# Attention weights: product with a diagonal of reciprocal sums instead of a multiplication and a transpose

## The reference

```
def _attend(q, parts, sink):
    scale = q.shape[-1] ** -0.5
    logits = []
    for k_, v_, bias in parts:
        s = jnp.einsum('bkgqd,bksd->bkgqs', q, k_).astype(jnp.float32) * scale
        if bias is not None:
            s = s + bias
        logits.append(s)
    ...
    p = jax.nn.softmax(jnp.concatenate(logits, axis=-1), axis=-1)
    out, off = None, 0
    for k_, v_, _ in parts:
        n = k_.shape[2]
        o = jnp.einsum('bkgqs,bksd->bkgqd', p[..., off:off + n].astype(v_.dtype), v_)
        out = o if out is None else out + o
        off += n
    return out
```

## Time and profile before

| | us |
|---|---|
| Median of 3 runs | 1862.6 (1861.91 to 1864.54) |
| The profiled execution, its own time | 1861.61 |
| Its span, first to last instruction | 1859.8 |
| TensorE busy | 1809.1 (97%) |
| DVE busy | 1341.2 (72%) |
| ACT busy | 981.0 (53%) |
| POOL busy | 178.7 (10%) |

### The profile page before, as it was taken

How to read it: one execution, slowest core, us unless ns; L and a number is a source line. 1 busy time by engine, 2 the same in 40 slices (tenths; PEclk the granted TensorE clock), 3 DMA queues, 4 the chain that set the end, 5 groups by cost and what they waited for, 6 DMA issues and landing times.

```text
span 1859.8 us, 27382 instructions
## 1 busy us (share of the span) xinstructions
PE 1809.1 (97%) x11100; PEld 1500.4 (81%) x11100; DVE 1341.2 (72%) x1973; ACT 981.0 (53%) x1470; POOL 178.7 (10%) x154
## 2 busy tenths in 40 slices
PE   5999999999999989999999999999999999999998
PEld 2988877797888767888977778888888786878888
DVE  3865677668897566998656688966765776769984
ACT  2754445545674454776344466744644445447663
POOL 2100121001000113000011210002100210020001
PEclk8999999999999999999999999999999999999999
DMA  9565656867555767665584766556655657645542
GB/s 368 191 233 200 204 215 227 313 230 282 235 195 189 267 223 294 246 228 199 186 303 171 292 271 264 188 184 249 227 183 190 233 179 281 237 163 200 192 176 86
DMA packets 72527, 418.12 MB, mean 225 GB/s; under 512 B 12176, under 2 KB 18696, under 8 KB 24144
## 3 DMA queue, kind: packets, MB, share of 16 engines
q1 hardware_dynamic: 54288, 392.98, 56.7%
q10 hardware_dynamic: 18112, 23.38, 3.9%
HBM read 405.35 MB, written 10.95 MB: 224 GB/s over the span
## 4 chain that ended last, share of the span: by engine, by line
PE 87%; DVE 5%; issue 2%; ACT 2%; DMA 2%; POOL 2%; POOLq 0%; DVEq 0%; ACTq 0%; SPq 0%
PE ps L586 18%; PE ps L608 9%; PE ps L643 9%; PE ps L589 9%; PE ps L568 6%; PE ps L624 5%; PE ps L646 4%; PE ps L571 3%; PE ps L685 3%; PE ps L554 3%; PE ps L556 3%; PE ps L555 3%; DMA raw<-in_stream 2%; PE ps L894 1%; PE ps L655 1%
## 5 line engine op out<-in xcount | busy, mean ns | idle before, releaser
L471 DVE TENSOR_TENSOR spl_lo<-raw,spl_hi 128x1024 fp32r<-128x1024 f32 x556 | 687.2, 1260 | 185.3 <-ACT spl_hi L460 184.2
L460 ACT ACTIVATE spl_hi<-raw 128x1024 fp32r<-128x1024 f32 x556 | 573.8, 1053 | 295.9 <-PE ps L646 111.0
L586 PE MATMUL ps<-H,spl_hi 128*128 128x512 f32 x1408 | 445.1, 398 | 3.4 <-DVE H L1760 3.4
L589 PEld LDWEIGHTS ps<-H,spl_lo 128*128 128x128 f32 x1408 | 265.2, 188 | 62.7
L589 PE MATMUL ps<-H,spl_lo 128*128 128x256 f32 x1408 | 277.2, 278 | 0.0
L586 PEld LDWEIGHTS ps<-H,spl_hi 128*128 128x128 f32 x1408 | 215.0, 189 | 14.6 <-issue 14.6
L643 PE MATMUL ps<-G,spl_hi 128*128 128x512 f32 x528 | 165.8, 395 | 0.0
L568 PE MATMUL ps<-B,spl_hi 128*128 128x512 f32 x512 | 160.9, 396 | 0.0
L554 PE MATMUL ps<-H,spl_hi 128*128 128x256 f32 x512 | 148.0, 289 | 6.0 <-DVE H L1760 4.5
L555 PE MATMUL ps<-H,spl_hi 128*128 128x256 f32 x512 | 145.8, 285 | 0.0
L556 PE MATMUL ps<-H,spl_lo 128*128 128x256 f32 x512 | 145.8, 285 | 0.0
(11 more groups left out here) (248 smaller groups left out, 2893.5 us busy)
## 6 DMA issues: line engine op xcount, KB each, us to landing
raw<-in_stream SPq DMA_DIRECT2D x374, 1024.0 KB, 4.9
out_new_C<-c_stage ACTq DMA_DIRECT2D x16, 512.0 KB, 3.8
ada_b<-in_ada_b ACTq DMA_DIRECT2D x4, 768.0 KB, 9.6
E<-rows_out ACTq DMA_DIRECT2D x8, 256.0 KB, 4.3
Em<-rows_out ACTq DMA_DIRECT2D x8, 256.0 KB, 4.6
x<-in_x ACTq DMA_DIRECT2D x1, 1024.0 KB, 11.9
wide<-rows_out ACTq DMA_DIRECT2D x8, 128.0 KB, 4.7
cache<-in_na_cache ACTq DMA_DIRECT2D x1, 1024.0 KB, 8.8
```

Source lines behind the costliest of these rows:

```text
L460: act.activation(spl_hi[m % SPL][:, :], raw[r % RAW][:, h * HALF:(h + 1) * HALF], ACT.Copy).then_inc(S["hi_done"], 1)
L471: dve.tensor_tensor(spl_lo[m % SPL][:, :], raw[r % RAW][:, h * HALF:(h + 1) * HALF], spl_hi[m % SPL][:, :].bitcast(F32), ALU.subtract).the ...
L586: pe.matmul(banks[:, b * 512:(b + 1) * 512], spl_hi[m % SPL][:, c], H[:, kk * 512:(kk + 1) * 512], start=kk == 0, stop=False, skip_group_c ...
L589: mm = pe.matmul(banks[:, b * 512:b * 512 + TOK], spl_lo[m % SPL][:, c], H[:, kk * 512:kk * 512 + TOK], start=False, stop=kk == KD - 1, sk ...
```

## The change

The division by the sums no longer happens in a pass over the weights. DVE writes `diag`, four 128 x 128 diagonal matrices with `rsum` of one head each on the diagonal (the identity, broadcast over four heads, times `rsum`, broadcast over 128 columns). `weights(u)` on TensorE replaces each transpose of a block of `Ea` by the matrix product of that block, as stationary operand, with the head's diagonal as moving operand: the block transposed, its columns scaled. GpSimd's part in attention is gone, and its semaphore `pn_done` is now raised by DVE. There is one `diag`, so the reciprocal of unit u waits also for `pt_mm`, the end of unit u-1's products on TensorE. `diag` takes 2 KB that nothing else used in attention.

```diff
--- before.py
+++ after.py
@@ -353,6 +353,7 @@
     vrow = sb("vrow", NS * D, F32, rA + 16 * KB)
     rope_t = sb("rope_t", 512, F32, rA + 28 * KB)
     rope_u = sb("rope_u", 512, F32, rA + 30 * KB)
+    diag = sb("diag", 4 * T, F32, rA + 26 * KB)
     qT = sb("qT", KD * TOK, F32, rB)
     kT = sb("kT", KD * 3 * T, F32, rB + 8 * KB)
     cache = sb("cache", 2 * D, F32, rB + 20 * KB)
@@ -971,8 +972,10 @@
                         pe.wait_ge(S["pt_d"], w // 2)
                     for b in range(1 + s):
                         for p in range(4):
-                            o = (4 * b + p) * T
-                            mm = pe.transpose(ACC[2 + b][:, p * T:(p + 1) * T], Ea[s][:, o:o + T], ident)
+                            c = 4 * b + p
+                            mm = pe.matmul(ACC[2 + b][:, p * T:(p + 1) * T], Ea[s][:, c * T:(c + 1) * T],
+                                           diag[:, c // (1 + s) * T:(c // (1 + s) + 1) * T], start=p == 0, stop=p == 3,
+                                           skip_group_check=True)
                     mm.then_inc(S["pt_mm"], 1)
 
                 def values(u):
@@ -2110,7 +2113,11 @@
                         link.wait()
                     if w:
                         dve.wait_ge(S["pn_done"], w)
+                        dve.wait_ge(S["pt_mm"], w)
                     dve.reciprocal(rsum[:, :], sums[:, :]).then_inc(S["rsum_done"], 1)
+                    dve.wait_ge(S["rsum_done"], w + 1)
+                    dve.tensor_tensor(v3(diag[:, :], T), ident.unsqueeze(1).to_broadcast([P, 4, T]),
+                                      rsum[:, :].unsqueeze(2).to_broadcast([P, 4, T]), ALU.mult).then_inc(S["pn_done"], 1)
 
                 def weights(u):
                     dve.wait_ge(S["pt_mm"], 8 * a + u + 1)
@@ -2386,13 +2393,6 @@
                         chain(pool.tensor_scalar(var[:, :], v3(mv[:, :], 2)[:, :, 1], 1.0, EPS, ALU.mult, ALU.add))
                         chain.wait()
                         pool.tensor_tensor(rstd[:, :], var[:, :], half_pow[:, :], ALU.pow).then_inc(S["root_done"], 1)
-                else:
-                    for u in range(8):
-                        width = (1 + u % 2) * T
-                        pool.wait_ge(S["rsum_done"], 8 * (i - 1) + u + 1)
-                        ev = v3(Ea[u % 2][:, 0:4 * width], width)
-                        pool.tensor_tensor(ev, ev, rsum[:, :].unsqueeze(2).to_broadcast([P, 4, width]),
-                                           ALU.mult).then_inc(S["pn_done"], 1)
                 norm(2 * i + 1)
 
             norm(2 * DEPTH, shift=False)
```

## The result

| | before | after |
|---|---|---|
| Median (6 runs each, same chip) | 1862.29 (1860.7 to 1864.84) | 1868.94 (1866.47 to 1872.4) |
| Ratio | | 1.0035 [1.0024, 1.0045] |
| The profiled execution | 1861.61 | 1872.4 |

The account below looks back on a forecast made before the run. TensorE was taken to bound the kernel, with a DVE and ACT chain pacing swa from about 665 to 693 us. swa +4.6 and na -0.7 gave +3.9 on the profiled execution, median 1866.5 us; stated range 1861.5 to 1870.

Parts of the forecast that it names:

- the forecast's own range: Whole kernel: 1864.7 to 1868.3 us, from the end of na 1 us either way and the diagonal 0.1 us.
- the case in which the clock falls: Rival, chance 0.25: TensorE's clock still falls at na's end, newly in swa, or both; 1867.7 to 1869.4 us.
- The product: TensorE, both layers: each transpose made a true product costs 0.114 us more, 10.9 us in all if nothing hides it.
- The rival of the four transposes: TensorE, both layers: a true product costs four transposes, 0.436 us, adding 20.3 us, total 1882.9; chance 0.02.
- The diagonal: DVE, 16 multiplications of 0.69 us, each moving what follows by about 0.73; swa's scores of unit 6 2.3 us later.
- The rival in which DVE's own waits hide the diagonals: swa: DVE's idle between units absorbs the diagonals, swa +0.8 us, total 1862.7, no change; chance 0.15.
- GpSimd gone: Both layers: weights ready 0.3 or 1.2 us sooner after the reciprocal; DVE regains 0.54, 0.39 and 0.58 us.
- The new wait: Reciprocal waiting for the previous unit's products: costs nothing in swa, about 0.25 us at unit 6 in na.
- the prediction's own sign: The prediction is wrong if a reciprocal waits for TensorE by more than 0.3 us in several units.
- The clock in swa: Rival's part for swa: the clock newly falls behind waits of 1.6, 1.3 and 1.4 us, costing 1.7; clock rival's chance 0.25.
- The main case: The forecast itself, chance 0.48: swa +4.6 us without a clock fall, na -0.7, total 1866.5 us.
- The end of na: Unit 7's products start 0.3 us sooner; the clock stays up, worth 1.7 us, of which 1.2 remain after tiles.

Follow-up runs that it names:

- e4: From the changed kernel: GpSimd instead of DVE writes the diagonal and takes the wait for the previous unit's products; 1865.52 us against 1862.69, ratio 1.0018.
- e3: From the changed kernel: TensorE transposes again, DVE still writes the diagonal but it is unused, softmax left undivided; 1862.05 us against 1862.69, ratio 1.0000.
- e5: From the changed kernel: five unread products on TensorE in each of two idle stretches of swa; 1866.93 us against 1863.69, ratio 1.0022.
- e8: From the kernel before: GpSimd's multiplication moved to DVE in na alone, transposes kept; 1861.35 us against 1863.69, ratio 0.9986.
- e2: From the changed kernel: two diagonal buffers in turn, so a reciprocal waits for the products of two units ago; 1868.55 us against 1862.69, ratio 1.0034.
- e10: From the kernel with DVE's multiplication in na alone: wide units multiplied in two halves, TensorE starting after the first; 1861.6 us against 1862.40, ratio 0.9997.
- e1: The changed kernel run and profiled again, nothing altered; 1869.55 us against 1862.69 for the kernel before, ratio 1.0036.
- e7: From the changed kernel: modulation tiles at the end of na transfer only half their data; 1869.1 us against 1863.69, ratio 1.0032.
- e11: The kernel before with GpSimd's multiplication moved to DVE in na alone, run again on another chip; 1861.05 us against 1862.40, ratio 0.9994.
- e6: From the kernel before: transposes of the weights become true products with the identity, GpSimd still multiplies; 1871.71 us against 1863.69, ratio 1.0038.
- e9: From the changed kernel: no diagonal or product; DVE multiplies the weights in place in both layers, TensorE transposes; 1864.68 us against 1862.40, ratio 1.0014.

## Why the prediction was right, and where it was not

The forecast was 1866.5 in a range to 1870, "slower" the likeliest side; measured 1868.94. That lies above the forecast's own range (1868.3) and inside the stated one only because this was stretched over the case in which the clock falls.

**The product: right.** 0.114 us more for each was taken from L788 against L794. Sixteen records take 1.87 to 1.98 us from start to start of what follows, 0.12 a record, so a product takes about twice the transpose's 0.11 to 0.13, and 20 of them cost 2.27 us in e4. The Trainium skill (TensorE: Matmul & The Clock Gate, Terms) has transpose mode four times faster for fp32. The runs show twice, for these operands as for L788's. The rival of the four transposes is out.

**The diagonal: right.** 0.69 us, and 2.5 us of chain up to the scores of unit 6 in e3, 2.38 in e5, against 2.3. The rival in which DVE's own waits hide the diagonals is out by the same number.

**GpSimd gone: right in kind.** nm is 0.16 to 0.17 everywhere. The 0.57 that na's block at 990 was to win is the step of -0.58 there in e8 and e3. In after it is -0.45: the block starts without idle, straight behind unit 1's products and values, so they did not quite fit before it; at the next scores the shift is -0.35.

**The new wait: right in what it costs.** By the prediction's own sign it was wrong, as three reciprocals wait for TensorE by more than 0.3 us (1.50 and 0.35 in swa, 0.5 for the forecast 0.25 in na); the 1.50 comes of the fallen clock, and in e5 that reciprocal does not wait. But e2 takes the wait away and wins 0.1 us. It costs nothing by itself in swa, and in na the idle before unit 7's products is 0.38 with it and 0.21 in e2 without.

**The clock in swa: the rival happened.** The main case counted swa without a fall. Its sum was right to 0.1 us in the run that held the clock (e5), and the fall came on top: 1.6 us at the scores of unit 3 (1.7 was the rival's price), 1.2 to 1.5 by the end of swa (58.98 and 59.28 less e5's 57.82). In e3, with as long idle stretches and without the product, the fall came too and cost 0.1 by the scores of unit 6, so its price is not fixed; idle time behind it can take it up. The rival had even foreseen the idle stretches, 1.6, 1.3 and 1.4 (measured 1.34, 1.26 and 1.04), and got no more than 0.25 of chance because "waits of nearly that size in swa before it left the clock alone". Those stood singly: before, the 1.13 was followed by 0.53 and not by 1.26. That they have to stand together is not shown. The weighing failed, not the mechanism, and e10 shows that even the old row of stretches was no safe evidence: one profile was read as what always happens.

**The end of na: the step that failed.** The prediction let the clock stay and TensorE's idle before unit 7's products shrink to 0.4, and both came: clock 1.00, idle 0.38. The products start only 0.07 us sooner than before, counted from na's first scores, not 0.3. Then the prediction took off only part for "the tiles themselves come some 0.8 later" and kept 1.2 us. Two waits took this gain. One is for tiles: 0.85 + 0.55 in after and 0.98 + 0.91 in e1. Before the change the transfers ran at 423 GB/s through TensorE's slow stretch; it was not free time to be won but time in which the next tiles landed. The other lies at the same place, hidden under the first tile wait: unit 7's `values` need `O_lo`, which DVE writes behind the diagonal, a weight split and a copy, a step that the working left out. It shows where no tile is late, 0.54 in e7 and 0.96 in e5. So smaller tiles (e7) take back 0.9 to 1.4 us and still leave na 0.6 over the forecast, and in e5, with no wait for a tile in that place, na is 1.06 over it.

**The next block**, +0.64 and +0.88, where the forecast had nothing. TensorE waits there for a tile that lands 21.7 us behind the end of na in after and 22.0 in e1, against 20.5 in e8, e10 and e11. The idle differs (1.16 and 2.92) because in after the clock fell ahead of it, as in before, and in e1 it did not. What makes this tile late stays open: halving the transfers at the end of na left it at 21.9 (e7), while e5, after's code from there on, has it at 20.6.

**The sum.** Over the one profile of before, 3.9 were forecast and the stages gave 7.4 in after and 7.3 in e1. The clock in swa is 1.5 and 1.2 of the difference, the end of na 1.5 and 2.0, the next block 0.6 and 0.9, less 0.2 and 0.7 by which the stretch between the layers came out shorter than in that profile. That stretch was as short (254.19) in e10, whose code there is before's, so it is chance in the reading and not a gain.

What decides whether the clock falls stays open. e4 kept it behind 0.62 and 0.53, e6 lost it behind 0.62, 0.53 and 0.72. Two pairs differ with the same code and the same stretches: before and e10 in swa, e8 and e9 (1.77) at the end of na.

## What to carry to other kernels

Replacing a pass over data on a slow engine by a matrix product pays only if TensorE is idle where the product runs and if the operand that it needs is not made on the engine that paces the chain; here TensorE had nothing idle in the last third of swa and DVE, which wrote the diagonal, paced the rest, while the plain multiplication on DVE in na alone took 1.5 us off that layer, of which the total showed 1.4 to 2.3, once clear of noise and once not. Before counting an idle stretch as a gain, see what the transfers did in it. See also which engine delivers last at its end. After each edit list TensorE's idle stretches anew: all six profiles in which those of swa grew (after, e1, e2, e3, e7, e9) lost the clock there. And one profile in which the clock held is no proof that it always does.

## What the runs showed of the hardware

- A product of 128 x 128 fp32 in two records loads its stationary operand in 192 ns per record, a transpose in 140 (one record); the pitch per record is 0.11 to 0.13 us for both.
- A fall of the granted clock from 1.00 to 0.50 (2.4 to 1.2 GHz) lasted 3 to 4 us. In swa it cost 1.2 to 1.5 us in after and e1, 1.36 in e10 and 0.1 in e3. It came behind stretches of 1.34 and 1.26 us and, in e10, behind 1.12, 0.53 and 0.73, which before had passed unharmed; one stretch of 1.77 at the end of na was followed by it in e9 and not in e8 and e11.
- Ten useless products in two idle stretches made swa 1.1 to 1.5 us shorter (57.82 in e5; 58.89 to 59.28 in after, e1, e2 and e7).
- The start of the kernel, the same code in all, varies by 3 us between executions (663.4 to 666.6 at swa's first scores), as much as half of what the change does.
